# Selected values moved to the first unit behind the first layer norm, half of it done one token tile at a time

## The reference

```python
x = layer_norm(DEEPNORM_ALPHA * x + y, ln_g[0], ln_b[0])
shared = shared_kv(x, kv_w, ...)

def shared_kv(h, kv_w, pos_k, w1_k, w2_k, pos_v, w1_v, w2_v):
    kv = (h @ kv_w).reshape(bsz, seq, 6, N_KV_HEADS, HEAD_DIM)
    k_c, v_c, k_s, v_s, k_w, v_w = [kv[:, :, i] for i in range(6)]

    def compress(t, pos, w1, w2):
        blk = t[:, idx] + pos[None, None, :, None, :]
        blk = jnp.moveaxis(blk, 3, 2).reshape(bsz, n_cmp, N_KV_HEADS, CMP_BLOCK * HEAD_DIM)
        return jax.nn.gelu(blk @ w1) @ w2

    return (compress(k_c, ...), compress(v_c, ...), k_s, v_s, k_w, v_w)
```

## Time and profile before

| | |
|---|---|
| median of 3 runs | 2034.88 us (2034.85 to 2035.08) |
| profiled execution, its own time | 2038.27 us |
| its span in the trace | 2036.5 us |
| granted TensorE clock over it | 0.997 |
| TensorE matmul busy | 2007.4 us (99%) |
| VectorE busy | 1307.7 us (64%) |
| ScalarE busy | 977.4 us (48%) |
| GpSimd busy | 80.0 us (4%) |
| DMA | 360.80 MB, mean 177 GB/s |

### The profile page before, as it was taken

One profiled execution on the slowest core, in us unless ns is written; L12 is line 12 of the kernel. 1 busy time (PEld: TensorE's weight loads), 2 busy tenths in 40 slices (PEclk: granted clock), 3 DMA queues, 4 the chain that ended last, 5 costly groups with the idle time before them and its releaser, 6 DMA issues.

```text
span 2036.5 us, 31846 instructions
## 1 busy us (share of the span) xinstructions
PE 2007.4 (99%) x12361; PEld 1770.0 (87%) x12361; DVE 1307.7 (64%) x1913; ACT 977.4 (48%) x1438; POOL 80.0 (4%) x84
## 2 busy tenths in 40 slices
PE   8999999999999999999999999999999999999998
PEld 7898899988989898889999988888888888888886
DVE  6799777466666666668757766555556555555555
ACT  5554454354455444445446446554344434434443
POOL 2000043000000000100000001000000000000000
PEclk9999999999999999999999999999999999999999
DMA  8334568545465555656554555566666666666663
GB/s 281 99 131 164 191 205 259 158 143 176 145 176 152 168 155 165 231 155 188 166 165 155 166 167 165 186 176 190 199 190 184 199 190 182 195 196 178 197 193 106
DMA packets 202935, 360.80 MB, mean 177 GB/s; under 512 B 25360, under 2 KB 33904, under 8 KB 202160
## 3 DMA queue, kind: packets, MB, share of 16 engines
q1 hardware_dynamic: 200656, 351.82, 56.4%
q0 software_dynamic: 1664, 5.97, 0.9%
q10 hardware_dynamic: 480, 1.10, 0.1%
HBM read 355.96 MB, written 2.10 MB: 176 GB/s over the span
## 4 chain that ended last, share of the span: by engine, by line
PE 89%; DVE 7%; ACT 2%; issue 2%; DMA 0%; ACTq 0%; POOL 0%; POOLq 0%; DVEq 0%
PE acc L518 36%; PE acc L522 18%; PE banks L518 8%; PE banks L1095 6%; PE acc L1095 6%; PE banks L1098 3%; PE acc L1098 3%; DVE w_high_low L1756 2%; PE acc L608 1%; PE banks L877 1%; PE banks L904 1%; ACT w_high_low L1139 1%; PE acc L549 1%; PE banks L890 1%; PE banks L983 0%
## 5 line engine op out<-in xcount | busy, mean ns | idle before, releaser
L1756 DVE TENSOR_TENSOR w_high_low<-raw,w_high_low 128x1024 fp32r<-128x1024 f32 x648 | 796.4, 1237 | 633.4 <-ACT w_high_low L1139 631.7
L1139 ACT ACTIVATE w_high_low<-raw 128x1024 fp32r<-128x1024 f32 x648 | 681.4, 1059 | 720.0 <-PE acc L518 323.4
L522 PE MATMUL acc<-x_high_low,w_high_low 128*128 128x256 f32 x3648 | 454.3, 285 | 0.7 <-issue 0.7
L522 PEld LDWEIGHTS acc<-x_high_low,w_high_low 128*128 128x128 f32 x3648 | 444.0, 192 | 2.9 <-issue 1.5
L518 PE MATMUL acc<-w_high_low,x_high_low 128*128 128x512 f32 x1728 | 414.4, 395 | 0.0
L518 PEld LDWEIGHTS acc<-w_high_low,x_high_low 128*128 128x128 f32 x1728 | 321.7, 188 | 66.5 <-issue 0.2
L518 PE MATMUL acc<-w_high_low,h_high 128*128 128x512 f32 x1088 | 292.7, 391 | 3.0 <-DVE w_high_low L1756 1.1
L518 PEld LDWEIGHTS acc<-w_high_low,h_high 128*128 128x128 f32 x1088 | 202.7, 188 | 46.0 <-issue 2.1
L518 PE MATMUL acc<-w_high_low,h_low 128*128 128x512 f32 x544 | 167.6, 389 | 0.0
L1095 PE MATMUL acc<-x_high_low,w_high_low 128*128 128x512 f32 x512 | 161.3, 396 | 1.5 <-DVE x_rows L2113 1.1
L1095 PE MATMUL banks<-x_high_low,w_high_low 128*128 128x512 f32 x512 | 160.8, 395 | 0.0
(11 more groups left out here) (359 smaller groups left out, 1606.2 us busy)
## 6 DMA issues: line engine op xcount, KB each, us to landing
raw<-in_b_w_in SPq DMA_DIRECT2D x128, 512.0 KB, 3.8
raw<-in_w_mlp_in SPq DMA_DIRECT2D x128, 512.0 KB, 3.7
raw<-in_w_mlp_out SPq DMA_DIRECT2D x128, 512.0 KB, 4.7
raw<-in_w_in SPq DMA_DIRECT2D x96, 512.0 KB, 3.9
raw<-in_kv_w SPq DMA_DIRECT2D x48, 512.0 KB, 4.4
raw<-in_a_w_in SPq DMA_DIRECT2D x32, 512.0 KB, 5.7
raw<-in_b_w_out SPq DMA_DIRECT2D x32, 512.0 KB, 4.8
raw<-in_w_out SPq DMA_DIRECT2D x32, 512.0 KB, 4.4
```

Source lines behind the costliest of these rows:

```text
L522: ins_ = nc.tensor.matmul(ACC[pair][:, m // 2, (m % 2) * TOK:(m % 2 + 1) * TOK], wa[:, k, j, m * P:(m + 1) * P], xa[:, kt + j, :], start=f ...
L1139: nc.scalar.activation(WH[:, s % SPLIT, :, :], RAW[:, s, :, :], ACT.Copy).then_inc(hi_ready, SLOTS + 1 if first_one else 1)
L1756: V.tensor_tensor(WL[:, k, :, :], RAW[:, p % SLOTS, :, :], WH[:, k, :, :].bitcast(F32), ALU.subtract).then_inc(lo_ready, SLOTS + 1 if isin ...
```

## The change

The selected values v_s become unit 0, in mode "rows"; k_c and v_c move back by one, to units 1 and 2; k_s takes the place of v_s in the odd slots of the mixed stage, in mode "cols" (`KV_COL`). The first four slots of unit 0 are done by token tile (`by_tile`): tile 0 of slots 0 to 3 between the turns 4 and 5 of tile 1, then tile 1 of slots 0 to 3 around the turns 6 and 7. Eleven `keep_busy` matmuls become six. ScalarE and VectorE take the portions of this layer norm in another order (`TILED`), ScalarE's `high` of slot 3 comes after portion 1 instead of portion 4, and VectorE's splits and `low` stand in a new order. TensorE waits for the first pass (`comp_dve` 1) at m0 and for the second at m8; before, it waited for both at m0. The second layer norm is as it was.

```diff
--- before.py
+++ after.py
@@ -74,2 +74,3 @@
 PORTIONS = [(0, 0, 4), (0, 4, 4), (1, 0, 2), (1, 2, 2), (1, 4, 4), (0, 8, 4), (1, 8, 4), (0, 12, 4), (1, 12, 4)]
+TILED = [(0, 0, 4), (0, 4, 4), (1, 0, 2), (1, 2, 2), (1, 4, 4), (0, 8, 4), (0, 12, 4), (1, 8, 4), (1, 12, 4)]
 
@@ -379,3 +380,3 @@
 
-    KV_COL = [0, 1, 2, None, 3, 4, 5]
+    KV_COL = [3, 0, 1, None, 2, 4, 5]
 
@@ -506,2 +507,5 @@
 
+    def portions(first):
+        return TILED if first == TR_X1 else PORTIONS
+
     @block.tensor
@@ -556,2 +560,21 @@
 
+        def tile_there(first, t, s):
+
+            for m, (t_, k0, width) in enumerate(portions(first)):
+                if t_ == t and k0 == 2 * s:
+                    pe.wait_ge(split_done, first + m + 1)
+
+        def by_tile(unit, group, t, s, first):
+
+            k = s % SPLIT
+            if t == 0:
+                pe.wait_ge(lo_ready, unit * SLOTS + s + 1)
+            tile_there(first, t, s)
+            for j in range(2):
+                for n, (xa, wa) in enumerate(((XH, WH), (XH, WL), (XL, WH))):
+                    ins_ = nc.tensor.matmul(PAIRS[group % 2][:, t, :], xa[:, 2 * s + j, t * P:(t + 1) * P], wa[:, k, j, :],
+                                            start=s == 0 and j == 0 and n == 0, stop=False)
+            if t:
+                ins_.then_inc(slot_used, 1)
+
         def tile_turn(first, n, rows=0):
@@ -560,3 +583,3 @@
             if t:
-                pe.wait_ge(tr_tmp, first + PORTIONS.index((0, 4 * b, 4)) + 1)
+                pe.wait_ge(tr_tmp, first + portions(first).index((0, 4 * b, 4)) + 1)
             pe.wait_ge(tile_rows, rows + 4 * t + b + 1)
@@ -783,16 +806,23 @@
         tiles_apart(U_AOUT + 1, (G_AOUT + 3) % 2, CB, True, HH, HL)
-        for n in range(6):
-            if n == 4:
-                keep_busy(G_KV, 7)
+        for n in range(4):
             tile_turn(TR_X1, n)
-        keep_busy(G_KV, 4)
-
-        def later_turns(s):
-            if s in (1, 3):
-                tile_turn(TR_X1, 6 + s // 2)
-
-        gemm(U_KV, G_KV, "cols", ready=tiles_ready(TR_X1), extras=later_turns)
+        keep_busy(G_KV, 6)
+        by_tile(U_KV, G_KV, 0, 0, TR_X1)
+        tile_turn(TR_X1, 4)
+        by_tile(U_KV, G_KV, 0, 1, TR_X1)
+        tile_turn(TR_X1, 5)
+        by_tile(U_KV, G_KV, 0, 2, TR_X1)
+        by_tile(U_KV, G_KV, 0, 3, TR_X1)
+        by_tile(U_KV, G_KV, 1, 0, TR_X1)
+        by_tile(U_KV, G_KV, 1, 1, TR_X1)
+        tile_turn(TR_X1, 6)
+        by_tile(U_KV, G_KV, 1, 2, TR_X1)
+        by_tile(U_KV, G_KV, 1, 3, TR_X1)
+        tile_turn(TR_X1, 7)
+        for s in range(SPLIT, SLOTS):
+            for t in range(NT):
+                tile_there(TR_X1, t, s)
+            tick(U_KV * SLOTS + s, s, "rows", G_KV % 2, 2 * s, False, s == SLOTS - 1, XH, XL)
         gemm(U_KV + 1, G_KV + 1, "cols")
         gemm(U_KV + 2, G_KV + 2, "cols")
-        pe.wait_ge(comp_dve, 2)
         pe.wait_ge(acc_free, G_KV + 2)
@@ -801,2 +831,4 @@
             kv_, s4 = divmod(n, 4)
+            if s4 == 0:
+                pe.wait_ge(comp_dve, kv_ + 1)
             pe.wait_ge(lo_ready, tau + 1)
@@ -809,3 +841,3 @@
             ins_.then_inc(slot_used, 1)
-            tick(tau + 1, (tau + 1) % SLOTS, "rows", (G_KV + 3) % 2, 2 * n, n == 0, n == SLOTS - 1, XH, XL)
+            tick(tau + 1, (tau + 1) % SLOTS, "cols", (G_KV + 3) % 2, 2 * n, n == 0, n == SLOTS - 1, XH, XL)
 
@@ -1413,3 +1445,3 @@
 
-            t, k0, width = PORTIONS[m]
+            t, k0, width = portions(first)[m]
             act.wait_ge(tr_full, first + 4 * t + k0 // 4 + (2 if t else 1))
@@ -1426,3 +1458,3 @@
             tile_turned(TR_X1, m, 0, 0, 16)
-            if m in (4, 6, 7):
+            if m in (1, 6, 7):
                 high(0)
@@ -1447,3 +1479,3 @@
                 else:
-                    act.wait_ge(acc_free, G_KV + n + 1)
+                    act.wait_ge(acc_free, G_KV + n + 2)
                 nc.scalar.activation(KVC[:, n, half, :, :, 0, 2 * b:2 * b + 2].rearrange("p i n h -> p h n i"),
@@ -1452,5 +1484,5 @@
         unit(ticks=SLOTS - 3)
+        unit(first=lambda: half_copy(U_KV, G_KV, VS[:, 0, :]))
         unit(first=lambda: kvc_high(0))
         unit(first=lambda: kvc_high(1))
-        unit(first=lambda: half_copy(U_KV + 2, G_KV + 2, KS[:, 0:2, :]))
 
@@ -1470,3 +1502,3 @@
         unit()
-        unit(first=lambda: (half_copy(U_KV + 4, G_KV + 3, VS[:, 0, :]), comp_rows()), extras=comp_hidden)
+        unit(first=lambda: (half_copy(U_KV + 4, G_KV + 3, KS[:, 0:2, :]), comp_rows()), extras=comp_hidden)
         unit(first=lambda: half_copy(U_KV + 5, G_KV + 4, flat(KW[:, 0:2, :])))
@@ -2184,3 +2216,26 @@
 
-        layer_norm(0, G_AOUT + 3, U_KV, TR_X1)
+        v.wait_ge(tile_full, 1)
+        tile_residual(0, 3, G_AOUT + 3, ALPHA)
+        v.wait_ge(rstd_rows, 1)
+        for c in range(4):
+            tile_normed(0, c)
+        low(0)
+        v.wait_ge(slot_used, SLOTS * U_KV)
+        tile_residual(1, 3, G_AOUT + 3, ALPHA)
+        tile_split(TR_X1, 0)
+        v.wait_ge(rstd_rows, 2)
+        tile_normed(1, 0)
+        tile_normed(1, 1)
+        low(0)
+        tile_split(TR_X1, 1)
+        low(0, 2)
+        tile_split(TR_X1, 2)
+        tile_split(TR_X1, 3)
+        tile_normed(1, 2)
+        tile_normed(1, 3)
+        for m in range(4, 7):
+            tile_split(TR_X1, m)
+        for m in range(7, 9):
+            low(0)
+            tile_split(TR_X1, m)
 
@@ -2202,3 +2257,3 @@
             pos = (PT[:, 0, 80:112], PT[:, 1, 96:128])[n]
-            v.wait_ge(slot_used, SLOTS * (U_KV + n + 1))
+            v.wait_ge(slot_used, SLOTS * (U_KV + n + 2))
             for k in range(4):
@@ -2206,3 +2261,3 @@
                 shift = pos[:, CSTRIDE * half:CSTRIDE * (half + 1)].unsqueeze(1).unsqueeze(1).to_broadcast([P, 2, TOK // CSTRIDE, CSTRIDE])
-                V.tensor_tensor(kv_pieces(KVS[:, 4 * n + k, :]), kv_pieces(ACC[(G_KV + n) % 2][:, b, :]), shift,
+                V.tensor_tensor(kv_pieces(KVS[:, 4 * n + k, :]), kv_pieces(ACC[(G_KV + n + 1) % 2][:, b, :]), shift,
                                 ALU.add).then_inc(kv_added if k < 3 else acc_free, 1)
@@ -2216,3 +2271,3 @@
             else:
-                v.wait_ge(acc_free, G_KV + n + 1)
+                v.wait_ge(acc_free, G_KV + n + 2)
             hi_, lo_ = (KVC[:, n, half, :, :, part_, 2 * b:2 * b + 2].rearrange("p i n h -> p h n i") for part_ in range(2))
@@ -2228,7 +2283,7 @@
         unit(ticks=SLOTS - 3)
+        unit(first=lambda: half_copy(U_KV, G_KV, VS[:, 1, :]))
         unit(first=lambda: kvc_add(0), extras=kvc_lows(0))
         unit(first=lambda: kvc_add(1), extras=kvc_lows(1))
-        unit(first=lambda: half_copy(U_KV + 2, G_KV + 2, KS[:, 2:4, :]))
         unit()
-        unit(first=lambda: half_copy(U_KV + 4, G_KV + 3, VS[:, 1, :]))
+        unit(first=lambda: half_copy(U_KV + 4, G_KV + 3, KS[:, 2:4, :]))
```

## The result

The changed kernel takes 2043.65 us, the median of 6 runs (2041.41 to 2044.35). The kernel before, in 6 runs beside them, has a median of 2036.26 us (2034.85 to 2038.35). The ratio is 1.003 with a 95% interval of [1.0019, 1.0040]: slower, by more than the 0.2% that tell it from no change, with the lower end of the interval just under them. The two medians lie 7.4 us apart. The forecast was 2039.6 us with a range up to 2042.0, so the median lies 1.7 us above the range. The profiled execution is the quickest of the six, 2041.41 us, with a span of 2039.6 us.

What follows compares the result with a forecast made beforehand. TensorE, busy 99% of the span, was taken as the bound. Layer norm stage -0.4, lost cover +3.1, GpSimd collisions +1.05 and +1.0 sum to +4.7 us on 2034.88: 2039.6 us, range 2036.4 to 2042.0.

Steps and rivals of the forecast that it cites:

- The median shown stands 3.4 us lower with the same work in it, so I put the difference on it: Whole kernel: adds the +4.7 us to the median of 2034.88 us instead of the profiled execution's 2038.27.
- The clock falls in the new waits: Rival, new TensorE waits: at 1.2 GHz one pair of mixed slots would cost 3.8 us more; chance 0.03.
- The layer norm stage, -0.4: Stage behind the layer norm: useful half slots displace five keep_busy matmuls, but waits stand there; -0.4 us left.
- The mixed stage, +3.1: Mixed stage: the second pass loses its cover; TensorE waits 1.4, 1.2 and 0.5 us at m4, m5, m7.
- the first collision, +1.05: Mixed stage's start: a GpSimd addition after m0 makes VectorE's low take 2.27 us instead of 1.23; +1.05 us.
- The second collision, +1.0: Mixed stage: GpSimd's additions after m4 and m6 meet VectorE's unbroken chain; between 0 and 2.2, taken as 1.0 us.
- Costed at nothing: Half copies of v_s and k_s, DMA loads of slots and GpSimd's results are covered: 0 us.
- The pass stays hidden: Rival, mixed stage: low of m4 to m7 comes in time, only the -0.4 stands, 2034.5 us; chance 0.10.
- No collision decides: Rival, mixed stage: GpSimd late at m0 or locked out throughout; +2.7 us, 2037.6 us; chance 0.15.
- Every collision: Rival, mixed stage and layer norm: all GpSimd collisions with VectorE happen; +6.6 us, 2041.5 us; chance 0.20.

Runs made afterwards that it cites:

- spread and GpSimd later: The change with ScalarE's second pass spread (two high, two kvc_high, one high, two kvc_high) and six GpSimd instructions eight slots later: 2034.64 us, ratio 0.9991.
- matmuls at taps 1: Kernel before plus 20 matmuls of unread result at the second group of taps, ahead of the wait for tap_blocks: 2035.97 us, ratio 0.9994.
- change again: The kernel of the change, unedited, run again beside the kernel before: 2043.95 us, ratio 1.0025.
- k_s slots first: The change with the mixed stage's 16 slots reordered: four k_s slots first, then w1 never more than twice in a row: 2038.84 us, ratio 1.0006.
- spread pass: The change with ScalarE's high of m4 ahead of the four kvc_high, high of m5 between the second and third: 2039.04 us, ratio 1.0008.
- m4's wait filled: The change plus 24 matmuls of 256 columns, result unread, ahead of m4 so TensorE doesn't stand still: 2042.76 us, ratio 1.0025.
- unit order only: The change's new unit order and mixed stage, but the layer norm's stage as in the kernel before: 2042.69 us, ratio 1.0028.
- change with matmuls at taps 1: The change plus the same 20 unread matmuls at the second group of taps: 2040.48 us, ratio 1.0017.
- GpSimd later: The change with six of GpSimd's x_rows instructions eight slots later, so that none falls between m0 and m6: 2040.44 us, ratio 1.0017.

## Why the prediction was wrong, and where it was right

**The step that failed: "The median shown stands 3.4 us lower with the same work in it, so I put the difference on it".** The 3.4 us are not the cost of profiling. They lie between two levels of the kernel before, and its own trace had the main cause of the upper one: clock 0.85, 0.50 and 0.80 from 96 to 108 us. From the taps to the first turn it takes 237.68 - 99.26 = 138.4 us, and 135.7 in the profile of spread and GpSimd later, where the clock is 1.00 (98.52 to 234.20): the dip costs 2.7 us. The other 0.7 is how much earlier that profile reaches the taps. The matmuls at taps 1 removed the upper level. Three runs that all fell on the lower level gave a base of 2034.88; the median over 103 runs is about 2037.6. The same sum on that base gives 2042.3, and what is measured is 2043.65 and 2043.95. This step alone is 2.7 of the 4 us by which the forecast was low. Of the other 1.3 the stages of the change again show 1.2: -0.74 + (37.33 - 30.65) = +5.9 us where +4.7 was forecast, 1.05 by the low clock and 0.5 by longer waits, less 0.3 that the layer norm stage gave beyond its forecast.

**The second: "The clock falls in the new waits" at 0.03, and 3.8 us.** It fell behind the wait at m4 in all four profiles in which that wait was 2.6 us and unfilled: to 0.50 for m4 or for m5. I had judged by the earlier trace rows that the clock was at 2.4 GHz behind 5.5 us of waiting. That reading was wrong, as TensorE's timeline of the kernel before tells:

```profile
8.99 5.83 PE L608 MATMUL acc<-x_cols,raw 128*128 128x256 f32 x16
...
23.42 3.62 PE L608 MATMUL acc<-x_cols,raw 128*128 128x256 f32 x16
```

The next matmuls start at 14.66 and 26.88, so the same 16 take 5.7 us here and 3.5 there: the first of them start 0.43 us apart, those after 13.5 us 0.22. The kernel begins at half pace, and the profile shows 1.00 up to there because its record of the clock begins at 13.5 us. The price was wrong too: 0.2 us at most in the first profile and 1.05 us in the second, since m5 and m7 wait for VectorE anyway.

**The size of the change.** Forecast +4.7 us. Measured: 4.5 us with the early dip filled on both sides; 0.25% or 5.1 us (0.16% to 0.34%, 3.3 to 6.9) for the change again; 5.6 us between the spans of the change again and of before, two profiles that have the same early dip; 6.3 us between the medians of their runs. The terms, each against a profile:

- *The layer norm stage, -0.4*: -0.74 (75.20 against 74.46). Slot 0 of tile 0 waited 0.16 us, and slot 4 waited 0.38 instead of 1.0. The rest of the plan held.
- *The mixed stage, +3.1, and the first collision, +1.05*: waits of 2.8, 1.2 and 0.5 us at m4, m5 and m7 in the first profile (m4 from the end of m3 at 316.27 + 2.87; for m7 without the low clock), in all 4.5; forecast were 1.4 + 1.05, 1.2 and 0.5. The 0.3 us more are at m4. m8 waited for nothing. That the pass had lost its cover is shown by k_s slots first and by the spread pass.
- *The second collision, +1.0*: there in the change again, in the filled one and in the unit order only (`kvc_low` 2.15 to 2.20 us), absent in the first profile and in the change with matmuls at taps 1. So it is 0 or 1.0 and not one value. The SBUF page's rule of the Trainium skill ("SBUF — State Buffer", section "Who interferes with whom"), by which both later ones would collide, did not hold: up to m7 at most one of the two made an instruction of VectorE longer, and the other waited (9.76, 3.98 and 4.44 us in three profiles).
- *Costed at nothing*: no wait for a half copy, a load or GpSimd's rows is seen behind m0.

**The rivals.** "The pass stays hidden" would need no wait at m4: there were 2.6 us. "No collision decides" is out, as GpSimd later took 1 us from the wait at m4. "Every collision", 2041.5, is near the median for other reasons: it has one collision more than was found and 2.7 us too little base.

**What goes with the two levels.** The start of the kernel differs between executions. Its first matmuls change from 0.43 to 0.22 us at 10.1 to 14.7 us, and the later they do, the later the taps are reached (97.63 to 99.87 us). Nine profiles have the wait of 2.47 us unfilled and nothing added ahead of it. In the order of that change of pace, the clock missing from 96 to 108 us adds up to 1.7 us at 10.1 (k_s slots first), 0 at 11.7 and 12.0 (pass spread; spread and GpSimd later), 3.4 at 12.7 to 13.5 (unit order only, m4's wait filled, change again, before), and 1.7 again at 14.3 and 14.7 (GpSimd later; the first profile of the change). The first turn comes at 234.1 to 234.7 us in the first three of them and at 236.8 to 237.7 in the other six, which are the two levels. So the same wait of 2.47 us is followed by the low clock or not, and in these nine it goes with how late the kernel came to full pace. Nobody varied that start, so it is an order seen in nine profiles and not a tested cause.

**What stays open.** What makes the start differ; and why the runs of the change with its early dip filled still lie up to 3.1 us apart, of which the two states of the mixed stage, 35.2 and 37.3, are an explanation that I did not test run by run.

## What to carry to other kernels

Before taking a median of three as the base, look in the profiled execution for a dip of the granted clock: its length times what is missing of 1.00 (3.4 us here) came near what it cost (2.7 us by the starts), other executions of the same kernel may not have it, and a prediction has to say on which level of the runs it stands. A clock of 1.00 at the start of a kernel is to be checked against the pace of its matmuls. A unit of short slots is no cover for a pass of ScalarE and VectorE that a unit of long ones hid; add up each engine's program order from the last event that both share. When a chain of VectorE sets the start of every second slot, other delays of TensorE in between, a low clock too, cost next to nothing until they outgrow its waits.

## What the runs showed of the hardware

**A wait of 2.5 to 2.6 us can be enough for the low clock.** It followed all four waits of 2.61 and 2.62 us ahead of m4, and the wait of 2.47 us ahead of the taps in seven of nine profiles, not in the other two. With matmuls in the wait it stayed at 1.00 at both places. Behind 1.60 us and less it was never seen in the mixed stage.

**GpSimd beside an unbroken chain of VectorE either goes in next or stays out for long.** In the chain of `low` and `kvc_low` behind v_c, GpSimd's additions and products that started 0.47 to 0.91 us after VectorE's running instruction (five, as the 323.63 against 323.16 above) went in next and made the next VectorE instruction 1.0 to 1.1 us longer. Ten that started 0.04 to 0.42 us after it stayed out for long and took 5.5 to 9.8 us in all, while VectorE kept its 1.22 and 1.1; the 7.26 us of the earlier trace rows are one of them. In the first profile of the change:

```profile
324.12 9.76 POOL L2836 TENSOR_TENSOR x_rows<-x_rows,gain_bias_half 128x512 f32<-128x512 f32 x1 [6.31 <-PE banks L839]
```

It started 0.21 us after the `kvc_low` at 323.91. The slower m4 of that run, at the end of which it starts, is what moved it there. That the place of its start decides is not shown, though. In the chain behind k_c of GpSimd later:

```profile
298.74 2.17 POOL L2835 TENSOR_TENSOR x_rows<-x_rows,gain_bias_half 128x512 f32<-128x512 f32 x1 [4.55 <-DMA gain_bias_half<-in_ln_b]
```

It started 0.21 us into a `low` (298.53), and the `kvc_low` behind that took 2.21 us. Five profiles have such a collision with a start 0.18 to 0.37 us in, and spread and GpSimd later has one at 0.33 that stayed out for 8.51 us. So what decides stays open.
